# A decoder step on Trainium2: where the page cache is read beside three stages of dense work

## What is computed

```python
def diff_attend(q, segments, q_pos, rel_bias, lam):
    for k, _, k_pos in segments:
        s = einsum('bqhmd,bkhmd->bmhqk', q, k) * scale
        logits.append(where(n >= 0, s + bias, -inf))
    p = softmax(concatenate(logits, -1), -1)
    attn = p[:, 0] - lam * p[:, 1]
    ... sum over segments of einsum('bhqk,bkhv->bqhv', attn, v)

def layer(x, attend, s0, chunk):
    dq, dk, dv, hq, hf, hi, hgate = split_proj(rmsnorm(x, norm1_w) @ w_in)
    o_da = rmsnorm(attend(q, k, v), da_subln_w) * (1 - lam_init)
    o_hg, s_new = hgrn2_mixer(hq, hf, hi, hgate, ...)
    x = x + concatenate([o_da, o_hg]) @ w_out
    x = x + hier_moe(rmsnorm(x, norm2_w), ...)      # 16 experts, 2 a token
```

## Time and profile before

| | us |
|---|---|
| median of 3 runs | 1408.94 |
| lowest and highest run | 1407.4 and 1412.66 |
| profiled execution, its own time | 1416.24 |
| its span, first to last instruction | 1414.4 |
| values stage, attention, output stage and its tail, in the trace | 538.9 to 629.2, 629.2 to 862, 862 to 1081.2 |

### The profile page before, as it was taken

One profiled execution on the slowest core, in us unless ns is written; L12 is line 12 of the kernel. 1 busy time (PEld: TensorE's weight loads), 2 busy tenths in 40 slices (PEclk: granted clock), 3 DMA queues, 4 the chain that ended last, 5 costly groups with the idle time before them and its releaser, 6 DMA issues.

```text
span 1414.4 us, 24197 instructions
## 1 busy us (share of the span) xinstructions
PE 1252.0 (89%) x9261; PEld 891.3 (63%) x9261; DVE 625.7 (44%) x1464; ACT 367.6 (26%) x756; POOL 123.0 (9%) x288
## 2 busy tenths in 40 slices
PE   6999997999999899987777878999896499999986
PEld 5666875667678788664455545455453387887852
DVE  4001316435364646465867766375525312121117
ACT  4021201211222224234554554222122011111113
POOL 4400000000000002020000000100000111111022
PEclk9999998999999999999898999999998599999998
DMA  8811001010020106669898899999970699999837
GB/s 256 287 52 31 30 30 45 31 43 19 3 90 2 61 0 225 202 240 321 283 314 280 287 303 334 345 324 334 306 251 19 198 312 301 296 300 298 277 127 293
DMA packets 158308, 274.03 MB, mean 194 GB/s; under 512 B 13448, under 2 KB 72752, under 8 KB 158208
## 3 DMA queue, kind: packets, MB, share of 16 engines
q1 hardware_dynamic: 139776, 217.46, 46.0%
q0 software_dynamic: 11648, 38.39, 7.7%
q10 hardware_dynamic: 6784, 16.85, 3.3%
HBM read 235.55 MB, written 37.09 MB: 193 GB/s over the span
## 4 chain that ended last, share of the span: by engine, by line
PE 71%; DVE 13%; SPq 5%; issue 4%; DMA 3%; ACT 3%; another core or an unknown queue 0%; POOL 0%; DVEq 0%; ACTq 0%; POOLq 0%
PE bank L1085 16%; PE bank L1088 13%; PE bank L1509 10%; PE bank L1368 5%; PE bank L1529 4%; DVE arena L1787 4%; PE bank L1134 4%; SPq L557 3%; PE bank L1213 3%; PE bank L1254 3%; DMA arena<-in_cache_k_dram 2%; PE bank L1320 1%; PE bank L1062 1%; PE bank L1298 1%; PE bank L1524 1%
## 5 line engine op out<-in xcount | busy, mean ns | idle before, releaser
L1085 PE MATMUL bank<-arena 128*128 128x352 f32 x768 | 239.3, 470 | 0.0
L1085 PEld LDWEIGHTS bank<-arena 128*128 128x128 f32 x768 | 147.4, 195 | 80.8 <-issue 6.6
L1088 PE MATMUL bank<-arena 128*128 128x256 f32 (+1 forms) x864 | 195.5, 384 | 0.6 <-issue 0.6
L1088 PEld LDWEIGHTS bank<-arena 128*128 128x128 f32 (+1 forms) x864 | 155.2, 183 | 33.1 <-issue 5.5
L1787 DVE STREAM_TRANSPOSE arena<-arena 128x512 f32<-128x512 f32 x256 | 156.1, 676 | 22.5 <-DMA arena<-in_cache_k_dram 22.2
L1509 PEld LDWEIGHTS bank<-arena 128*128 128x128 f32 x1024 | 143.2, 193 | 9.2 <-issue 9.2
L1509 PE MATMUL bank<-arena 128*128 128x160 f32 x1024 | 144.3, 302 | 1.9 <-DVE arena L2099 1.9
L1368 PE MATMUL bank<-arena 128*128 128x512 f32 x256 | 118.3, 605 | 0.9 <-ACT arena L910 0.9
L1213 PE MATMUL bank<-arena,tab 128*32 128x256 f32 x1024 | 69.2, 416 | 33.9 <-DVE arena L1787 24.9
L766 ACT ACTIVATE arena<-bank 128x352 f32<-128x352 f32 x48 | 22.3, 464 | 234.2 <-PE bank L1085 234.2
L1368 PEld LDWEIGHTS bank<-arena 128*128 128x128 f32 x256 | 46.5, 192 | 53.3 <-issue 53.1
(11 more groups left out here) (342 smaller groups left out, 1485.0 us busy)
## 6 DMA issues: line engine op xcount, KB each, us to landing
arena<-in_cache_k_dram SPq DMA_DIRECT2D x256, 256.0 KB, 5.0
arena<-in_cache_v_dram SPq DMA_DIRECT2D x256, 256.0 KB, 4.0
arena<-in_expert_w_dram SPq DMA_DIRECT2D x48, 1024.0 KB, 8.3
arena<-in_w_in_dram SPq DMA_DIRECT2D x14, 1024.0 KB, 5.1
expert_scratch<-route POOLq DMA_DIRECT2D x40, 256.0 KB
expert_scratch<-arena ACTq DMA_DIRECT2D x16, 512.0 KB
out_dram<-arena SPq DMA_DIRECT2D x12, 512.0 KB, 3.0
arena<-in_x_prompt_dram SPq DMA_DIRECT2D x4, 1024.0 KB, 9.1
```

The costliest lines, as they stand in the source:

```text
L1085: mm = nc.tensor.matmul(bank(g)[:, 0:N3], w[:, k, c * P:(c + 1) * P], hT[:, k * TOK + n * N3:k * TOK + (n + 1) * N3], start=(k == 0), stop ...
L1088: mm = nc.tensor.matmul(bank(g)[0:ROWS[c], 0:256], tok(hT, k, c), w[:, k, :], start=(k == 0), stop=(k == KC - 1))
```

## The change

Three tables are changed, and the residual rows are issued one at a time.

```diff
-        v_beat = [0, 0, 0, 0, 0, 0, 0, 0, 2, 4, 5, 7, 9, 10, 12, 14, 16, 18]
+        v_beat = [0, 0, 0, 0, 2, 4, 6, 8, 10, 12, 14, 16, 18, 20, 22, 24, 26, 28]
...
-            return (4.5 - i) * 0.44 + 60 / len(units)
+            return (4.5 - i) * 0.44 + 52 / len(units)
...
-        u_beat = [v_beat[-1] + round(60 * sum(pages_of[:k + 1]) / sum(pages_of)) for k in range(len(parts))]
+        u_beat = [v_beat[-1] + round(52 * sum(pages_of[:k + 1]) / sum(pages_of)) for k in range(len(parts))]
...
-        rows_at = sum(name in "KV" for t, name, b, g in steps if t <= u_beat[-1]) + QUADS + 1
+        taken = sum(name in "KV" for t, name, b, g in steps if t <= u_beat[-1]) + QUADS + 1
+        row_at = {taken + (BEATS - u_beat[-1]) * (i - 2) * 4 // 30 + (i > 2) * 4: i for i in range(2, 8)}
...
-                            if q == rows_at:
-                                residual_rows()
+                            if q in row_at:
+                                residual_rows(row_at[q])
...
-            def residual_rows():
-                sp.wait_ge(sem("p_used"), cumT[(H - 1, 7, 4)])
-                sp.wait_ge(sem("out"), 32)
-                for i in range(2, 8):
-                    sp.dma_start(x1[i], xp_v[:, i, :]).then_inc(sem("x1_more"), 16)
-                for c in range(4):
-                    sp.dma_start(x_smp[32 * c:32 * c + 32, :], xs_v[:, c * 256:c * 256 + 256]).then_inc(sem("x1_more"), 16)
+            def residual_rows(i):
+                if i == 2:
+                    sp.wait_ge(sem("p_used"), cumT[(H - 1, 7, 4)])
+                    sp.wait_ge(sem("out"), 32)
+                sp.dma_start(x1[i], xp_v[:, i, :]).then_inc(sem(f"x_in{i - 2}" if i < 7 else "x1_more"), 16)
+                if i == 7:
+                    for c in range(4):
+                        sp.dma_start(x_smp[32 * c:32 * c + 32, :], xs_v[:, c * 256:c * 256 + 256]).then_inc(sem("x1_more"), 16)
...
-                if n == 0 and i == 2:
-                    dve.wait_ge(sem("x1_more"), 160)
+                if n == 0 and i >= 2:
+                    dve.wait_ge(sem(f"x_in{i - 2}" if i < 7 else "x1_more"), 32 if i < 7 else 80)
```

More of the change, by code:

```diff
@@ L580, in _ @@
             sp.wait_ge(sem("x1_in"), 32)
-            sp.wait_ge(sem("x1_more"), 160)
+            for i in range(5):
+                sp.wait_ge(sem(f"x_in{i}"), 32)
+            sp.wait_ge(sem("x1_more"), 80)
             sp.wait_ge(sem("wout_in0"), 64)
```

## The result

The changed kernel takes 1446.42 us (median of 4 runs, 1441.56 to 1451.06) where the kernel before, run beside it, takes 1410.8: ratio 1.0244, 95% interval 1.0215 to 1.0274. It is **slower**, and outside the forecast range. The profiled execution took 1441.56 us.

The account below looks back on a forecast made before the run. The attention was taken as bound by TensorE and VectorE handing work to each other, not by delivery. +10.3 + 1.7 - 13.8 - 3.2 = -5.0 turned the median 1408.9 into 1404 us, range 1389 to 1419.

Parts of the forecast that it names:

- Matmul work: All stages: values gains 11.0 us of matmul work, attention loses 9.0, output loses 1.9; nothing in sum.
- The first keys, +10.3: Values stage: TensorE's first K pair, after the fifth projection, waits 10.3 us for VectorE to turn its pages.
- The clock, +1.7: Behind the first-keys stall: half clock slows TensorE's work, costing 1.7 us, with bounds 0 and 5.
- I count no further stall: Values stage after the first K pair: page turning and the ring keep ahead, so no more waits, 0 us.
- 0.85 us a quad; eight fewer give -6.8: Attention: 51.1 us of TensorE idle time spread over 60 quads; eight fewer quads save 6.8 us.
- Nothing gained (0): Attention: one bound of the idle-time term, 0 us, the idle time only moving; the other bound was -28.2.
- V pages at the start of the attention, -3.9: Start of the attention: the first V quads are fetched and used before, so TensorE's 3.9 us wait goes.
- Residual rows, -3.2: Output stage: issuing the rows singly instead of in a block removes TensorE's 3.2 us wait near it.
- Slower, 1417: Rival: attention idle time stays, as VectorE's page turning meets units of 384 to 640 columns; 1417.7 us, chance 0.21.
- Delivery was the bound: Rival: page transfers bound the kernel, so the whole stream moves up by 12.4 us; 1396.5 us, chance 0.12.
- The mixture pays: Rival: in the attention, half of the 21.4 us idle in light-unit stretches vanishes besides, -10.7; 1393 us, chance 0.27.
- The clock: Rival: the stall at the first keys costs 5 us of slowed clock instead of 1.7; 1407 us, chance 0.08.

Follow-up runs that it names:

- late: The changed kernel with its first K pair after the ninth value projection instead of the fifth, attention tables untouched; 1.0251 of the kernel before.
- take_now: The changed kernel with ScalarE copying each K pair's scores in the pair's own step instead of one step later; 1.0144 of the kernel before.
- only_att: The kernel before with 52 instead of 60 attention beats, eight quads moved to the output stage, residual rows single; 1.0162 of the kernel before.
- first_half: The changed kernel with each head's quads in the units of 768 and 896 columns put into the unit's first half; 1.0156 of the kernel before.
- defer_after: The changed kernel, turning K pages behind the second causal bias part where the second next unit has 640 columns or more; 1.0186 of the kernel before.
- defer_before: The kernel before, turning K pages behind the second causal bias part where the second next unit has 640 columns or more; 0.9949 of the kernel before.
- defer_rows: The kernel before with single residual rows and page turning deferred behind the second causal bias part; 1407.28 us, 0.9945 of the kernel before.
- rows_only: The kernel before with its old tables and only the residual rows issued one by one; 0.9992 of the kernel before.
- tables_only: The changed tables with the residual rows in one block as in the kernel before; 1.0273 of the kernel before.
- phase22: The changed kernel with 64 instead of 52 attention steps, twelve quads moved there from the output stage; 1.0134 of the kernel before.
- experiment 2: Two runs: late, the changed kernel with a later first K pair, 1.0251; only_att, the kernel before with 52 attention beats, 1.0162.
- take_late: The changed kernel with the first K pair after the ninth projection and each pair's scores copied in its own step; 1.0163 of the kernel before.
- first_half_all: The changed kernel with quads in the first half, scores copied in the pair's step and page turning deferred; 0.9988 of the kernel before.

## Why the prediction was wrong, step by step

- **Matmul work**: right in what moved. The values stretch has 291 matmuls more, which is two K pairs and six V quads of 32 each, 64 + 192, and the 35 of a softmax. What the attention's eight quads cost there can't be read from the busy time, which rose while the work fell.
- **The first keys, +10.3**: right in size (10.4 us, against the wait above). But taking the stall away gained nothing on the whole: late saved 6.7 us in the stretch and gave 5.4 back in the next, 4.1 of them in TensorE's busy time.
- **The clock, +1.7**: right for the one stall. Behind it the granted clock was 0.50 (1.2 GHz) from 562 to 566 us. The first pair took 3.64 us where a pair at full clock takes 1.93, and the projection after it 0.2 more:

```profile
562.28 3.64 PE L1217 MATMUL bank<-arena,tab 128*32 128x256 f32 x32 [10.44 <-DVE arena L1791]
565.85 3.94 PE L1092 MATMUL bank<-arena 128*128 128x256 f32 x16
570.78 1.94 PE L1217 MATMUL bank<-arena,tab 128*32 128x256 f32 x32 [0.99 <-ACT arena L830]
```

  That is 1.9 us, not the 5 us of a whole stretch at half clock. As a term it was too narrow: I looked for the clock behind one wait, and it was lost in the attention, where no wait is over 4.0 us.
- **"I count no further stall"**: the step that failed in the values stage. I had checked VectorE's turning and SyncE's ring, not ScalarE, whose copy of each pair stood behind the next projection's copies. Six waits of 1.2 us and a top chain that started late: 13.6 us by take_now, where 0 was written. The stretch came to +34.9 instead of +23.0.
- **"0.85 us a quad; eight fewer give -6.8"**: failed. Idle time was divided by quads as if each brought its own. A V quad between scores and flips covers a wait; taking it away uncovers it. only_att, with the values stage untouched, has 55.0 us of idle time with eight quads fewer.
- **"Nothing gained (0)" as the upper bound of the attention**: failed. The bound excluded a loss, without a reason that did. Idle time came to 49.6 us instead of 37.3 (12.3 more), and the clock (0.94 to 0.87) made the work take 191.3 us where 183.4 - 9.0 = 174.4 was due (17 more). Together they are the 29 us by which the attention was missed. By an estimate from the two mean clocks, 174.4 x 0.94 / 0.87 = 188.4, some 14 of the 17 go with the clock and 3 stay open. I kept the busy time of the earlier trace rows as a fixed quantity; it isn't one.
- **What lengthened it**: the quads that rounding moved behind the wait they covered (7.4 us by first_half), page turning between two bias parts (8.2 by defer_after, but 7.6 in the kernel before too), and the clock. It came back to 0.93 with defer_after; with first_half it is 0.89, no more than profiles of the same attention differ by (0.95 and 0.93 in defer_before and defer_rows). The half of the unit stood in the tables that set the order, and I had read only how many quads a unit has.
- **V pages at the start of the attention, -3.9**: part right. Their wait fell from 3.9 to 2.3 us. **VectorE's waits for K pages, -3.1**: wrong in sign, they rose from 4.4 to 9.2 us.
- **Residual rows, -3.2**: failed. The single rows take that wait away (0.2 us near the place in rows_only), but the stretch keeps 8.0 of its 9.0 us of waiting for page turning, and the whole time shows nothing (0.9992). The new tables take the wait away with the block in place (tables_only). The output stretch gained 10.5 us, 5.4 more than forecast: the wait of key matmuls for turning went from 9.0 to 0.4 us there. only_att, with eight quads more there, lost 20, 2.5 us a quad, and phase22, with twelve fewer, gained 20.8 on the changed kernel, 1.7 a quad, against 1.1 of matmul work (9.0 / 8). Why was not tried.
- **Costs put at nothing**: held. No wait of TensorE on GpSimd's query copies is listed in the attention.
- **The rivals.** *Slower, 1417* named the right sign, and its condition was met: the attention gave back only 1.5 us of idle time (51.1 to 49.6), and the prediction's own sign of being wrong, 50 us of idle time, came. Its mechanism was not what ran: the wait of key matmuls for turning halved, the scores waited for the bias instead, and this order costs the kernel before as much. It also kept the busy time fixed and the values stage as forecast, so it came out 29 us low. *Delivery was the bound* fell: the attention's DMA share went down to 0.75 and the time up. *The mixture pays* fell with experiment 2. *The clock* was priced on the stall alone.

## What to carry to other kernels

Work of another kind inside a latency chain is cover as well as cost: before counting what fewer pieces save, mark at each piece which wait it stands in front of, by its place and not by its number. Check every engine that a moved step touches, the one that only copies its result too. And never carry a busy time over to another order as it is: the same work in another order can run at a lower granted clock, here with 17 us on 174.

## What the runs showed of the hardware that was not expected

- The granted clock of a whole stage moved with the order of work alone: 0.94, 0.87, 0.84, 0.90 and 0.94 in the attentions of before, after, take_late, only_att and first_half_all, with idle time between 45 and 55 us in all of them. Defer_after has the idle time of the changed kernel (50.1 and 49.6 us) at 0.93 instead of 0.87, and the 8.2 us that it is shorter are all busy time. Profiles of the same attention differ by up to 0.02. So here the sum of the waits did not set the clock; what in their lengths and places did was not tried by itself.
- The start of the values stretch varies by 8.5 us between profiles of kernels that are alike up to there.
